# Slots of four score pieces instead of two in the attention stage, and the first head's banded keys loaded during the projections

## What is computed

```python
# A: 8 heads, 2 shared K/V groups; three branches per head, merged by sigmoid gates
s_cmp = q @ k_cmp.T * scale - slope * dist        # 63 compressed blocks
p_cmp = masked_softmax(s_cmp); o_cmp = p_cmp @ v_cmp
# selected blocks: top 16 of 16 blocks of 64 keys, that is all causal keys
o_slc = masked_softmax(q @ ks.T * scale - slope * dist, dist >= 0) @ vs
# banded: the last 512 keys
o_win = masked_softmax(q @ kw.T * scale - slope * dist, 0 <= dist < 512) @ vw
o = g0 * o_cmp + g1 * o_slc + g2 * o_win
# B: 4 heads, softmax(q k' * scale + cum_t - cum_s) v, causal, with a cumulative log forget gate
# C: 4 heads, p = softmax_0 - lambda * softmax_1 of two 32-wide maps each, causal; then an RMSNorm per head
x = x + concat(A, B, C) @ w_out
x = x + top-2-of-8 experts inside the top-1 of 4 groups (32 experts of width 256)
out = RMSNorm(x)
```

## Time and profile before

| | us |
|---|---|
| median of 3 runs (lowest, highest) | 1369.82 (1365.38, 1373.25) |
| the profiled execution, its own time | 1367.83 |
| its span in the trace | 1365.9 |
| its mean granted TensorE clock | 0.924 |

### The profile page before, as it was taken

One profiled execution on the slowest core, in us unless ns is written; L12 is line 12 of the kernel. 1 busy time (PEld: TensorE's weight loads), 2 busy tenths in 40 slices (PEclk: granted clock), 3 DMA queues, 4 the chain that ended last, 5 costly groups with the idle time before them and its releaser, 6 DMA issues.

```text
span 1365.9 us, 22552 instructions
## 1 busy us (share of the span) xinstructions
PE 1194.6 (87%) x8298; PEld 866.5 (63%) x8298; DVE 626.0 (46%) x1567; ACT 399.1 (29%) x716; POOL 199.1 (15%) x447
## 2 busy tenths in 40 slices
PE   1899899996998999999989899929999999999840
PEld 1889788775776878888767688724444444444310
DVE  3330344233564676665675423363343434343327
ACT  5221112221353555444765222201111111111102
POOL 3020000001211111211542100010000000000024
PEclk8899999998797999999998999959999999999975
DMA  7010744355256445544534333173999999999527
GB/s 300 32 47 32 253 154 139 139 169 139 64 118 209 102 113 127 121 102 110 166 108 141 140 112 101 68 332 128 367 369 366 366 369 375 361 367 371 201 100 285
DMA packets 71484, 261.60 MB, mean 192 GB/s; under 512 B 20929, under 2 KB 29409, under 8 KB 61793
## 3 DMA queue, kind: packets, MB, share of 16 engines
q1 hardware_dynamic: 59584, 217.37, 48.2%
q0 software_dynamic: 7056, 25.69, 5.0%
q10 hardware_dynamic: 4752, 17.30, 3.1%
HBM read 206.71 MB, written 53.48 MB: 190 GB/s over the span
## 4 chain that ended last, share of the span: by engine, by line
PE 77%; DVE 9%; DMA 6%; issue 3%; SPq 2%; POOL 2%; ACT 1%; ACTq 0%; POOLq 0%; DVEq 0%
PE PS L1943 16%; PE PS L1671 11%; PE PS L1818 9%; PE PS L1958 8%; PE PS L1883 7%; PE PS L1660 5%; PE PS L1762 4%; PE PS L1798 4%; PE PS L1799 3%; PE PS L1935 2%; DMA k<-T_d 2%; PE PS L1792 2%; DMA q<-shr 1%; POOL y L838 1%; DMA wst<-in_wt 1%
## 5 line engine op out<-in xcount | busy, mean ns | idle before, releaser
L1943 PE MATMUL PS<-wgu,XT 128*128 128x512 f32 x512 | 227.9, 598 | 4.0 <-DVE XT L1554 3.1
L997 ACT ACTIVATE pt<-PS,cst 128x512 f32<-128x512 f32 (+3 forms) x288 | 172.3, 650 | 173.6 <-PE PS L1799 139.6
L1303 DVE CUSTOM_DVE_ANT_0 junkm<-PS,cst 128x512 f32<-128x512 f32 (+3 forms) x276 | 136.9, 532 | 101.9 <-PE PS L1762 99.0
L1943 PEld LDWEIGHTS PS<-wgu,XT 128*128 128x128 f32 x512 | 98.1, 192 | 127.9 <-issue 125.6
L1818 PE MATMUL PS<-V,pt 128*64 128x65 f32 x3840 | 160.2, 236 | 0.0
L1818 PEld LDWEIGHTS PS<-V,pt 128*64 128x64 f32 x3840 | 136.2, 147 | 35.2 <-issue 23.2
L1958 PE MATMUL PS<-wdn,aT 128*128 128x512 f32 x256 | 115.4, 593 | 1.9 <-ACT aT L850 1.9
L1762 PE MATMUL PS<-k,q 128*128 128x128 f32 (+3 forms) x336 | 95.6, 363 | 20.3 <-DMA k<-T_d 13.3
L771 POOL TENSOR_SCALAR_AFFINE_SELECT pt<-pt 128x128 f32<-128x128 f32 x224 | 67.6, 305 | 273.6 <-ACT pt L997 225.8
L1671 PE MATMUL PS<-hTh,wth 128*128 128x512 f32 x256 | 102.6, 401 | 4.5 <-DVE wtl L1153 4.5
L1559 DVE TENSOR_SCALAR ge<-PS 128x256 f32<-128x256 f32 x32 | 13.6, 425 | 200.3 <-PE PS L1943 200.3
(11 more groups left out here) (272 smaller groups left out, 1774.9 us busy)
## 6 DMA issues: line engine op xcount, KB each, us to landing
wgu<-in_wgu SPq DMA_DIRECT2D x33, 2048.0 KB, 11.0
wdn<-in_wdn SPq DMA_DIRECT2D x33, 1024.0 KB, 13.1
Y_d<-YO ACTq DMA_DIRECT2D x33, 512.0 KB, 2.6
q<-T_d SPq DMA_DIRECT2D x60, 256.0 KB, 4.9
k<-T_d SPq DMA_DIRECT2D x60, 256.0 KB, 5.6
wst<-in_wt SPq DMA_DIRECT2D x16, 512.0 KB, 6.4
T_d<-thi SPq DMA_DIRECT2D x16, 512.0 KB, 2.6
T_d<-tlo SPq DMA_DIRECT2D x16, 512.0 KB, 3.9
```

Source lines behind the costliest of these rows:

```text
L997: ins = nc.scalar.activation(pt[:, (n + 2) % 6, 0:nt * P], PS[:, n % 4, 0:nt * P], ACT.Exp, scale=C("slopes", h, h + 1), bias=C("kb", w, w ...
L1303: V_.tensor_tensor_reduce(out=junk_[:, n % 2, 0:L], in0=PS[:, bank, 0:L], in1=tab, scale=1.0, scalar=-3e38, op0=ALU.add, op1=ALU.max, accu ...
L1943: ins = mm(PS[:, 2 + p, :], XT[:, p, c, :], wgu[q][:, c, :], start=(c == 0), stop=(c == KC - 1))
```

## The change

Slots hold four pieces and up to four maxima, in turns; the values run one slot behind, not two; the transpose of a unit's maxima stands in the slot just ahead of its scores (three slots ahead for a C unit), behind that slot's first piece; VectorE does the output batches last in a slot. `pt` has 8 buffers. The banded keys of unit 2 get a tile of their own, `K1y`, loaded during the projections, and its maxima use the first unit's queries (the same head's) with it, so that only `Q2` and `K2` are loaded for it later. The tile `maskc` moves, and `wraw` is loaded at f == 18. There are 95 slots.

```diff
-    LEAD, DEEP = 9, 2
+    PER, LEAD, DEEP, BUFS = 4, 4, 1, 8
...
-                    at_ = 1 + k // 3 if n == 2 else slot - self.LEAD + k // 2
+                    at_ = slot - self.LEAD + k // self.PER
                     self.m_at.setdefault(at_, []).append((x, k))
-                self.tp_at.setdefault(at_ + 1, []).append(x)
+                self.tp_at.setdefault(slot - (3 if x.kind == "C" else 1), []).append(x)
             for k, (c, *_) in enumerate(x.s):
-                self.s_at.setdefault(slot + k // 2, []).append((x, k))
+                self.s_at.setdefault(slot + k // self.PER, []).append((x, k))
                 if k + 1 == len(x.s) or x.s[k + 1][0] != c:
-                    self.out_at.setdefault(slot + k // 2 + self.DEEP + 1, []).append((x, c))
-            slot += len(x.s) // 2
+                    self.out_at.setdefault(slot + k // self.PER + self.DEEP + 1, []).append((x, c))
+            slot += (len(x.s) + self.PER - 1) // self.PER
...
-        junka, junkm = (at(n, [P, 2, 512], f32, o) for n, o in (("junka", ZD + 32 * KB), ("junkm", ZB + 48 * KB)))
+        junka, junkm = at("junka", [P, 512], f32, ZD + 32 * KB), at("junkm", [P, 2, 512], f32, ZB + 48 * KB)
+        K1y = at("K1y", [P, SEQ], f32r, ZD + 34 * KB)
...
-        pt = at("pt", [P, 6, 512], f32, ZE + 12 * KB)
-        maskc = at("maskc", [P, SEQ], f32r, ZE + 8 * KB)
+        pt = at("pt", [P, 8, 512], f32, ZE + 8 * KB)
+        maskc = at("maskc", [P, SEQ], f32r, ZD + 40 * KB)
...
                 for dst, half, part, r0 in ((Q1, 0, 0, q0), (Q1, 1, 1, q0), (K1, 0, 0, k0), (K1, 1, 0, k0),
-                                            (Q2, 0, 0, q0), (K2, 0, 1, k0)):
+                                            (Q2, 0, 0, q0), (K2, 0, 1, k0))[4 * (x.n == 2):]:
...
             load_unit(PLAN.full[0])
+            sp_.wait_ge(act_did, AC.of("c1v"))
+            sp_.wait_ge(pe_did, PEV.of("ov"))
+            sp_.wait_ge(t_st[1], 32 * 5 + 1)
+            for half in range(2):
+                sp_.dma_start(K1y[HD * half:HD * half + HD, :].bitcast(f32), T_r[0, G_KW * P:G_KW * P + HD, :])\
+                   .then_inc(ky_in, 16)
...
-                if f and x.kind == "X":
-                    shift_row(PLAN.units[x.n + 1])
...
                     stored += 1
+                if f and x.kind == "X":
+                    shift_row(PLAN.units[x.n + 1])
...
-                if f == 4:
+                if f == 18:
                     for c in range(4):
                         sp_.dma_start(wraw[:, 2 * c:2 * c + 2, :],
...
             for slot_ in SLOTS:
-                if slot_ == 6:
+                if slot_ == 3:
                     settled()
                     augment(1)
                     augment(2)
...
                 if n == 4:
-                    act.wait_ge(t_st[1], 32 * 8 + 1)
-                if n >= 6:
-                    act.wait_ge(pv_done, n - 5)
+                    for p in range(2):
+                        act.wait_ge(t_st[p], 32 * 8 + 1)
+                if n >= PLAN.BUFS:
+                    act.wait_ge(pv_done, n - PLAN.BUFS + 1)
...
             for slot_ in SLOTS:
-                for x, c in PLAN.out_at.get(slot_, ()):
-                    out_batch(x, c)
-                for x in PLAN.tp_at.get(slot_ - 1, ()):
+                for x in PLAN.tp_at.get(slot_, ()):
                     shift_rows(x)
                 for x, k in PLAN.m_at.get(slot_, ()):
                     maxima(x, k)
                     if k + 1 == len(x.m):
                         shift(x)
+                for x, c in PLAN.out_at.get(slot_, ()):
+                    out_batch(x, c)
...
+            def operands(x):
+                q1, k1 = (Q1[3], K1y) if x.n == 2 else (Q1[x.set], K1[x.set])
+                return q1, Q2[x.set], k1, K2[x.set]
...
-                if k == 0 and x.kind != "C":
-                    pe_.wait_ge(ld_in[s], 96 * ((PLAN.full.index(x) - 1) // 3 + 1 if x.n else 1))
+                if k == 0 and x.n == 2:
+                    pe_.wait_ge(ky_in, 32)
+                elif k == 0 and x.kind != "C":
+                    pe_.wait_ge(ld_in[s], loaded(x))
...
             for slot_ in SLOTS:
-                for x, k in PLAN.s_at.get(slot_, ()):
-                    scores(x, k)
-                for x, k in PLAN.m_at.get(slot_, ()):
-                    max_pass(x, k)
+                s_, m_ = PLAN.s_at.get(slot_, []), PLAN.m_at.get(slot_, [])
+                for k in range(max(len(s_), len(m_))):
+                    if k < len(s_):
+                        scores(*s_[k])
+                    if k == 0:
+                        for x in PLAN.tp_at.get(slot_, ()):
+                            shift_T(x)
+                    if k < len(m_):
+                        max_pass(*m_[k])
                 for x, k in PLAN.s_at.get(slot_ - PLAN.DEEP, ()):
                     values(x, k)
-                for x in PLAN.tp_at.get(slot_, ()):
-                    shift_T(x)
```

More of the change, by code:

```diff
@@ L130, in __init__ @@
         for t in range(self.end):
+            for x in self.tp_at.get(t, ()):
+                x.tp_use = use
+                use += 1
             for x, k in self.m_at.get(t, ()):
                 x.m_use = [*(x.m_use if k else []), use]
-                use += 1
-            for x in self.tp_at.get(t, ()):
-                x.tp_use = use
                 use += 1
@@ L393, in program @@
         z_in = sem("z_in")
+        ky_in = sem("ky_in")
         ld_in = [sem(f"ld_in{u}") for u in range(4)]
@@ L634, in _ @@
                     stored += 1
+                if f and x.kind == "X":
+                    shift_row(PLAN.units[x.n + 1])
+                if f and PLAN.full[f - 1].kind in "YF":
                     if stored == NSA_H + FOX_H:
@@ L786, in settled @@
             def settled():
-                pool.wait_ge(k_ready, sum(x.masked(k) is not None for t in range(6) for x, k in PLAN.s_at.get(t, ())))
+                pool.wait_ge(k_ready, sum(x.masked(k) is not None for t in range(3) for x, k in PLAN.s_at.get(t, ())))
             for slot_ in SLOTS:
-                if slot_ == 6:
+                if slot_ == 3:
                     settled()
@@ L1282, in maxima @@
                 n, b = x.m_use[k], x.n % 3
-                junk_ = junka if x.n < 2 else junkm
+                junk_ = junka[:] if x.n < 2 else junkm[:, n % 2, :]
                 bank = M_BANK[n % 2]
                 dve.wait_ge(m_ready, n + 1)
-                if n >= 2:
+                if x.n < 2 and n:
+                    dve.wait_ge(mx_done, n)
+                elif n >= 2:
                     dve.wait_ge(mx_done, n - 1)
                 if x.kind == "C":
-                    chain(V_.tensor_tensor(out=junk_[:, n % 2, :], in0=PS[:, bank, :], in1=C("distc"), op=ALU.add))
-                    V_.tensor_reduce(out=mx[:, b, 0, :], in_=junk_[:, n % 2, :].rearrange("p (t c) -> p t c", t=NT),
+                    chain(V_.tensor_tensor(out=junk_, in0=PS[:, bank, :], in1=C("distc"), op=ALU.add))
+                    V_.tensor_reduce(out=mx[:, b, 0, :], in_=junk_.rearrange("p (t c) -> p t c", t=NT),
                                      axis=AX.X, op=ALU.max).then_inc(mx_done, 1)
@@ L1302, in maxima @@
                     tab = C("dist", off, off + L)
-                V_.tensor_tensor_reduce(out=junk_[:, n % 2, 0:L], in0=PS[:, bank, 0:L], in1=tab, scale=1.0,
+                V_.tensor_tensor_reduce(out=junk_[:, 0:L], in0=PS[:, bank, 0:L], in1=tab, scale=1.0,
                                         scalar=-3e38, op0=ALU.add, op1=ALU.max,
@@ L1759, in max_pass @@
                 t, c, k0, nk = x.m[k]
-                q_, k_ = (Q2[s][0:96], K2[s][0:96]) if x.kind == "D" else (Q1[s][:], K1[s][:])
+                q_, k_ = (q2[0:96], k2[0:96]) if x.kind == "D" else (q1[:], k1[:])
                 edge = x.kind == "F" and k0 + nk == t + 1
@@ L1780, in scores @@
                     pe_.wait_ge(aug_set[s], 2)
+                    if x.n == 2:
+                        pe_.wait_ge(ld_in[s], loaded(x))
                 if k == 0 and x.kind == "C":
@@ L1791, in scores @@
                 if x.kind == "D":
-                    ins = mm(o, K2[s][0:97, j * P:(j + 1) * P], Q2[s][0:97, q], start=True, stop=True)
+                    ins = mm(o, k2[0:97, j * P:(j + 1) * P], q2[0:97, q], start=True, stop=True)
                 elif x.kind == "C":
                     mm(o, identr[:], maskc[:, q], start=True, stop=False)
-                    mm(o, kc1[:, HD * x.g:HD * x.g + P], Q1[s][:, q], start=False, stop=False)
-                    ins = mm(o, kc2[0:97, HD * x.g:HD * x.g + P], Q2[s][0:97, q], start=False, stop=True)
-                else:
-                    mm(o, K1[s][:, j * P:(j + 1) * P], Q1[s][:, q], start=True, stop=False)
-                    ins = mm(o, K2[s][0:HD + 1, j * P:(j + 1) * P], Q2[s][0:HD + 1, q], start=False, stop=True)
+                    mm(o, kc1[:, HD * x.g:HD * x.g + P], q1[:, q], start=False, stop=False)
```

(6 more changed lines are left out.)

17 lines of the change are left out of this document (11 added, 6 removed).

## The result

| | before | after |
|---|---|---|
| median (lowest to highest), 4 runs each on one chip | 1367.60 (1364.96 to 1373.25) | 1398.88 (1396.36 to 1402.72) |
| ratio, 95% interval | | 1.0236 [1.0198, 1.0274] |
| profiled execution, its own time | 1367.83 | 1402.72 |
| its span and mean granted clock | 1365.9, 0.924 | 1400.7, 0.917 |

The forecast was 1377 with a range of 1345 to 1396: the right sign, and the time outside the range. Three runs of the experiments were slow ones (1389.7 and 1389.3 us with VectorE's order undone, 1425.3 with the values between the pairs); the ratios leave them out, the medians do not. The page of the changed kernel, as of before: busy time of each engine, then the strips.

A forecast was written before the change was run, and what follows sets the result against it. TensorE was taken to set the attention stage's length, each stop costing twice through half clock. Start -11, heads -5, F +16, D +7 gave +7 on 1367.8, 1375, forecast as 1377 against the runs' median; range 1345 to 1396.

The forecast's parts named there:

- The start: Start of attention: the 10.7 us wait for unit 2's loads goes, a stop of 4 to 5 us comes; -11 us.
- Turns: TensorE's slots: each merged pair saves two turns, 0.24 us; -10 us in seven heads, -3 in F, -6 in D.
- Rows a slot ahead: Rows transposed one slot ahead reach their scores late: +24.5 us in seven heads, +2 in F, +14.5 in D.
- the X rows: Next head's X unit: VectorE casts its row late, after four maxima and both C batches; 2.5 us late per head.
- What goes with the old order: Old stops vanish: C stops 8 us over seven heads, F-load waits 1.5 in heads and 1 in F, D 9.
- Maxima: Four maxima in a row wait on VectorE's pace: 0.4 us per head, 0.8 per D unit; +3 and +5.6 us.
- The weights: Output projection's loads at f == 18: the heads' stop goes, -15 us; F3's row waits behind them, +19 in F.
- Clock: Half clock behind stops: 8 us go with the heads' old weights stop; short stretches there cost 12 instead of 10.
- Rival 3: Clock decides: stops of 1 us or more behind Y and D rows lower it too; 1396 us, chance 0.14.
- the first (rows less late): Rival: Y, F and plain D rows come in time, X rows 1 us late; 1347 us, chance 0.22.
- The fourth: Rival: only the start gains; turns cost nothing, and rows are in time or stops balance; 1365 to 1370, chance 0.12.

The follow-up runs named there:

- the values between the pairs: Changed kernel with output batches first and C's first batch one slot later, plus values run between pairs of score piece and maximum: 1396.79 us, 1.0199.
- the version with the weights spread: Changed kernel with output batches first, C's first batch one slot later, and `wraw`'s four loads one each at f = 16 to 19: 1344.91 us, 0.9822.
- the kernel with two pieces and all edits: Kernel before with `K1y` early, `wraw` loads one each at f = 4 to 7, differential end one operation per slot over four slots: 1339.85 us.
- the version with everything: Changed kernel, batches first, C's first batch one slot later, `wraw` loads one each, first three differential heads' ends in VectorE's gaps: 1335.01 us, 0.9759.
- scores, then maxima: Changed kernel, batches first, C's first batch one slot later, `wraw` loads one each; TensorE's slot order as in the kernel before: 1390.86 us, 1.0169.

## Why the prediction was wrong, point by point

- **The start** (-11): -10, and the wait on `k<-T_d` is 4.3 us at 341, as worked out. The part alone measured -10.8. Right.
- **Turns** (-10, -3, -6): this step failed. The price of a pair, 0.24, agrees with the values between the pairs (0.25), but merging slots didn't give it back. Busy time of the heads times their clock is 193 us before and 196 after, 195.2 in the version with the weights spread and 195.6 in the kernel with two pieces and all edits (the two rows above): none of the 10 is seen. In F some 1 us is: 52.1 us busy for the version with everything against 52.9 before, both at clock 1.00. In D nothing: 84.9 at clock 1.00 against 91.6 at 0.93, which is 85.2 at full clock. A part of it went into stops: a matmul behind a wait on a maximum takes 0.34 us to the next one (486.66 to 487.00 with the weights spread), a running one 0.24, and the heads have 35 such waits where the kernel before had 7. That is some 3 us by estimate; the rest is open.
- **Rows a slot ahead** (+24.5, +2, +14.5): in the seven heads and in F before the weights rows cost nothing, not 24.5 and 2; one of 0.5 us lies in the first head. In D they came near my number: 8.3 us ahead of scores and 5.8 ahead of maxima behind late casts, 14.1 against 14.5. The three behind a `diff_end` were 2.9, 2.9 and 3.3, worked out 3.1 each; the 5.0 is one row, issued at 685.77, 2.9 us after its cast and behind `ot<-O_d`, where I had 1.3 for each of four plain rows: that this sum fits is luck. The way is shorter than 3.5 from the cast, as one late row shows, the last of D (cast on VectorE, score on TensorE):

```profile
774.93 0.28 DVE L1339 CAST shr<-PS 8x128 fp32r<-8x128 f32 x1
777.03 2.08 PE L1818 MATMUL PS<-q,k 97*128 97x512 f32 x4 [3.30 <-DMA q<-shr]
```

The row took 2.1 us from its cast. The estimate of 3.0 that I had made with the Trainium skill (DMA: Bandwidth & Descriptors, Anatomy of one DMA), whose figure was measured for DMAs issued from GpSimd, was nearer than my 3.5. That the X rows came in time has another reason besides: VectorE was as late as I had it, its batches ended at 500.13, 7.0 us into the slot from 493.11 (worked out: 7.2), but TensorE had been held by them already, and its transpose came only at 500.99. My own mark for "wrong", waits on `q<-shr` under 20 us, was met: 18.4, 9.6 of them ahead of F3.
- **The output banks** (no term, so nothing): the step whose mechanism failed, in the sentence "Behind the casting VectorE stand only maxima". I had VectorE's four maxima, then both batches, until 7.2 us. I followed them to one user, the row's cast, and not to the other, the bank that the next values need. In the place of the late X rows stand 24.9 us of waits in the eight heads, 21.7 in the seven. The order undone alone (-27) and done alone (+51) show it from both sides.
- **What goes with the old order** (-8 for the C stops and the rest): right; no wait ahead of a C unit's maxima is left.
- **Maxima** (+3, +5.6): 4.6 us in the heads and 4.6 in D. Right.
- **The weights** (-15, +19): the 6.8 went, and the wait came ahead of F3 at 9.6 (worked out: 11), with half clock behind. F grew by 11.4 against +16. Right in mechanism. The row issued last came last, and with 1 MB at a time the longest wait on a row in the stage was 0.6. The Trainium skill's rule on the order within one queue (DMA: Bandwidth & Descriptors, Queues, rings and completion order) agrees with both.
- **Clock** (-8 with the old stop, +2 in the heads): too low. The heads had 39 us at half clock before and 44 after, since the new stops took the place of the one behind the weights; with the order undone the mean is 0.98. Rival 3 had the mechanism, at other stops. Besides, D went from 0.93 to 0.88, where I had +2.

The sum was +7 against +31 to +35. The waits for the banks that I did not have (21.7 in the seven heads) and the waits on rows that did not come (24.5) nearly cancel, and that is luck: 17.5 of the 24.5 were VectorE's lateness for the X rows, which TensorE met a step earlier and at another price. What separates the forecast from the time is above all 19 us for turns, of which about 1 showed, and the clock of the heads, which I had 6 us better and which came out 2.5 worse. The rivals: the condition of the first (rows less late) held and its time, 1347, did not, because it shared these terms; the third's time, 1396, was nearest, with stops of another origin. None named the bank. The fourth held that turns bring nothing; that part came out, its time did not.

## What to carry to other kernels

When an order on a helping engine is changed, list every buffer which that engine frees in the moved step, and ask for each who waits for it in the same slot; one consumer followed to the end is not enough. Then judge a set of stops by their length and the clock behind them as well as by their sum: about 25 us of waits in the heads ran at a clock of 0.98 where the longest was 1.8 us, and at 0.91 where seven were 2.36. A price measured for adding turns is not yet what taking them away gives. A large load ahead of a small one in a queue is best cut and spread over several turns, not moved as a block to another place.

## What the runs showed of the hardware that was not expected

- Two VectorE operations on tiles in SBUF, 0.69 and 0.78 us by themselves, took 1.73 and 1.75 us beside a GpSimd `tensor_tensor` on 128 x 512 float32, of which two took 2.95 us there against 1.28 for one elsewhere. A maximum of two 128 x 4 tiles in SBUF took 0.80 beside such a step and 0.16 without; one that reads PSUM kept its 0.69. The first of the two started 0.09 us behind the GpSimd step of 1.28 and took 1.04 more than alone. The Trainium skill (SBUF — State Buffer, Who interferes with whom) says that a VectorE operation with both inputs in SBUF contends with GpSimd's reads, the one that comes second being blocked; these rows agree.
- The same stops, 2.36 us once per head, were followed by different amounts of half clock: in the changed kernel by 10 us behind that at 498.30 and by none behind those at 466.47 and 534.68, and in two kernels that are equal up to there the first C unit began 3.0 us later in one and F 3.4 us earlier. Length alone doesn't decide: stops of 1.8 us at a maximum were followed by half clock in three of eight heads (VectorE's order undone), stops of 1.2 to 1.5 ahead of a C unit's maxima in five of seven (two pieces, all edits), and with scores, then maxima, the clock stayed full from 364 to 696 us with no stop over 1.35. What makes the difference stays open; a stop's price in clock is known only within some microseconds.
- The busy time of a values matmul of one form is 34 ns in groups of a whole slot and 44 in groups of one or two pieces. The Trainium skill (TensorEngine Tiling (Array Packing), Key Properties) says that a change of the tiling mode drains TensorE; the runs give an estimate of what leaving and coming back costs, 0.25 us, without showing that a drain is what it pays for.
